# A hybrid encoder block with 32 experts: another order for the last two experts, a routing table built in groups, and shorter first loads

## What is computed

```python
u = rmsnorm(x, g_mix); z = u @ w_in
a = pool_mixer(z[..., :512]); s = ssm_mixer(z[..., 512:])      # pooling heads, S5 heads with a scan
h = x + concat([a, s]) @ w_out
# mixture of experts: 4 groups of 8, best group, then two experts of it, weights w1 and w2
v = rmsnorm(h, g_ffn); combine = route(v)
for e in range(32):
    hg = silu(v @ w_gate[e]) * (v @ w_up[e]) * combine[:, e]
    h = h + hg @ w_down[e]                                     # 1024 -> 256 -> 1024
gate = sigmoid(rmsnorm(h, g_ple) @ ple_gate_w + ple_gate_b)    # 1024 x 1024
h = h + gate * (p @ ple_proj_w)
out = rmsnorm(h, g_final)
```

## Time and profile before

| | us |
|---|---|
| three runs | 503.12, 504.16, 507.57 (median 504.16) |
| the profiled execution, its own time | 504.42 |
| its span, first to last instruction | 502.5 |
| TensorE busy | 471.3 (94%) |
| VectorE busy | 232.4 (46%) |
| ScalarE busy | 167.8 (33%) |
| GpSimd busy | 150.5 (30%) |
| mean granted TensorE clock | 0.993 of full speed |

### The profile page before, as it was taken

The page is one execution under the profiler, slowest core; times in us unless marked ns, Lnnn a source line. Parts: engine busy times, 40 slices in busy tenths (PEclk is TensorE's granted clock), DMA queues, the critical chain, the costliest instruction groups (busy, mean ns, idle before and its releaser), DMA issues.

```text
span 502.5 us, 7271 instructions
## 1 busy us (share of the span) xinstructions
PE 471.3 (94%) x2722; PEld 259.3 (52%) x2722; DVE 232.4 (46%) x683; ACT 167.8 (33%) x280; POOL 150.5 (30%) x136
## 2 busy tenths in 40 slices
PE   3899999999999999989999999998999997999993
PEld 3445564644944467655555555554554453444441
DVE  2899969999233348652222222221112111665525
ACT  5633657557342333111111111121212111214554
POOL 1069999925110001222222222211121210004350
PEclk9999999999999999999999999998999999999998
DMA  8884300599399976899999999999999999990022
GB/s 295 158 205 93 73 0 1 199 115 229 137 332 417 420 327 226 319 397 422 420 418 417 419 416 412 421 418 419 420 420 419 417 421 358 400 372 2 0 83 83
DMA packets 59659, 144.73 MB, mean 288 GB/s; under 512 B 26594, under 2 KB 36358, under 8 KB 47336
## 3 DMA queue, kind: packets, MB, share of 16 engines
q1 hardware_dynamic: 54024, 133.92, 72.3%
q0 software_dynamic: 5328, 10.31, 5.3%
q10 hardware_dynamic: 272, 0.04, 0.0%
HBM read 138.17 MB, written 14.19 MB: 303 GB/s over the span
## 4 chain that ended last, share of the span: by engine, by line
PE 69%; DMA 19%; SPq 4%; issue 3%; DVE 2%; ACT 1%; POOLq 0%; POOL 0%; DVEq 0%
PE bank L1666 63%; DMA ring<-in_exp_w_up_dram 12%; DMA moe<-v_d,gidx_all 4%; SPq L390 3%; PE bank L2079 2%; DMA pairs_d<-moe,sidx_all 1%; PE bank L1764 1%; DMA big<-pairs_d 1%; PE bank L2098 1%; PE bank L1936 1%; PE bank L2196 1%; SPq L395 1%; DVE h L1419 1%; ACT moe L558 1%; PE bank L1754 0%
## 5 line engine op out<-in xcount | busy, mean ns | idle before, releaser
L1666 PE MATMUL bank<-ring,moe 128*64 128x256 f32 (+2 forms) x848 | 110.8, 406 | 2.9 <-DMA ring<-in_exp_w_up_dram 2.5
L1666 PEld LDWEIGHTS bank<-ring,moe 128*64 128x64 f32 x848 | 60.2, 138 | 39.4 <-issue 14.4
L1592 POOL DMA_INDIRECT pairs_d<-moe,sidx_all x32 | 31.8, 993 | 150.4 <-ACT moe L558 78.2
L935 DVE TENSOR_TENSOR vrow<-moe,bank 64x128 f32<-64x128 f32 x64 | 18.6, 291 | 111.9 <-ACT moe L834 110.9
L1666 PE MATMUL bank<-ut,big 128*128 128x512 f32 x128 | 57.7, 597 | 1.4 <-ACT ut L570 1.4
L558 ACT ACTIVATE moe<-bank 128x512 f32<-128x512 f32 (+1 forms) x65 | 36.5, 582 | 62.3 <-PE bank L1666 52.2
L834 ACT ACTIVATE moe<-bank 64x256 f32<-64x256 f32 x32 | 12.1, 378 | 131.6 <-PE bank L1666 124.6
L1666 PE MATMUL bank<-ring,ut 128*128 128x512 f32 x128 | 55.7, 593 | 0.2 <-DVE ut L935 0.2
L1666 PE MATMUL bank<-big,moe 128*64 128x256 f32 (+1 forms) x264 | 41.8, 427 | 2.5 <-DMA big<-in_exp_w_up_dram 2.1
L935 DVE TENSOR_TENSOR ring<-ring,bank 128x64 f32<-128x64 f32 (+1 forms) x142 | 39.4, 278 | 2.8
L1666 PEld LDWEIGHTS bank<-ring,ut 128*128 128x128 f32 x128 | 24.0, 190 | 29.1 <-issue 29.1
(11 more groups left out here) (200 smaller groups left out, 607.9 us busy)
## 6 DMA issues: line engine op xcount, KB each, us to landing
ring<-in_exp_w_gate_dram SPq DMA_DIRECT2D x19, 1024.0 KB, 28.5
ring<-in_exp_w_down_dram SPq DMA_DIRECT2D x18, 1024.0 KB, 25.0
ring<-in_exp_w_up_dram SPq DMA_DIRECT2D x17, 1024.0 KB, 29.9
big<-in_exp_w_up_dram SPq DMA_DIRECT2D x7, 1024.0 KB
big<-in_exp_w_down_dram SPq DMA_DIRECT2D x7, 1024.0 KB, 15.1
big<-in_exp_w_gate_dram SPq DMA_DIRECT2D x6, 1024.0 KB
ut<-in_exp_w_up_dram SPq DMA_DIRECT2D x4, 1024.0 KB, 17.8
h<-in_exp_w_down_dram SPq DMA_DIRECT2D x4, 1024.0 KB, 27.8
```

The lines of the kernel that those rows point to most:

```text
L935: return dve.tensor_tensor(o, a, b, op)
L1592: pool.indirect_dma_start(pairs, bass.IndirectOffsetOnAxis(ap=index, axis=0), at(moe, ALL, M_Y + k * 512, [[1, 512]]), None, bounds_check= ...
L1666: return pe.matmul(o, a, b, start=start, stop=stop, skip_group_check=loose)
```

## The change

Head: the identity alone (128 columns) is loaded after the second tile of `x`, the other 497 columns of the constants after the second half of `w_in`, under `ld_win1`. C is turned after its own four loads; the vectors have a semaphore of their own and are turned after the next product. The filling of `tbl_d` and the cast of `pair_i` move behind the pooling loops on GpSimd.

Table: `table_groups()` stands after 3 slices of expert 0's gate-up product, with the operands exchanged (32 columns of `rh` are the weights, 128 of `oh` move) and four column groups of one bank as targets; VectorE copies the 128 x 128 result to memory, and `table_folded()`, after 5 slices, adds the four groups by one product with a 0/1 matrix. VectorE builds `oh` between its two copies of expert 0's rows. GpSimd takes the bounds of its indirect DMAs from two registers that are set once, before it waits for the indices.

Last experts and tail: see the diff.

```diff
-        ORDER = [(0, 0), (0, 1)] + [x for e in range(NE - 1) for x in ((e + 1, 0), (e + 1, 1), (e, 2))] + [(NE - 1, 2)]
+        ORDER = ([(0, 0), (0, 1)] + [x for e in range(NE - 2) for x in ((e + 1, 0), (e + 1, 1), (e, 2))]
+                 + [(NE - 2, 2), (NE - 1, 0), (NE - 1, 1), (NE - 1, 2)])
...
-                    sp.dma_start(cst[:, :], A["consts"]).then_inc(ld_c, 16)
+                    sp.dma_start(at(cst, ALL, C_ID, [[1, P]]), dr(A["consts"], C_ID, [[C_END, P], [1, P]])).then_inc(ld_c, 16)
...
+            def load_first_pairs(n):
+                sp.dma_start(at(big, ALL, n * 512, [[DM, 2], [1, 512]]),
+                             dr(pairs_d, n * 512, [[2 * DM, P], [DM, 2], [1, 512]])).then_inc(ld_late_half if n else ld_pairs[0], 16)
...
             sp.wait_ge(gu_ps, NE - 1)
             load_gate(0, 0, 4, ld_wple)
-            sp.wait_ge(moe_done, 1)
-            sp.wait_ge(gu_ps, NE)
-            load_pairs(0)
             sp.wait_ge(dn_ps, NE - 1)
             load_gate(0, 4, 4, ld_wple)
             load_h(1)
+            sp.wait_ge(moe_done, 1)
+            load_first_pairs(0)
+            load_first_pairs(1)
+            sp.wait_ge(gu_ps, NE)
             load_pairs(1)
...
-            x_out(0, xT_sb, 2, V_FB)
+            x_out(0, xT_sb, 2, V_FB, (0,))
             tt(qv("oh", ...), ...).then_inc(place_done, 1)
+            x_out(0, xT_sb, 2, V_FB, (1,))
...
             dve.wait_ge(tbl_ps, 1)
-            seq(dve.tensor_scalar(at(tblw, ALL, 0, [[1, NE]]), bank[6][:, 0:NE], float(EMPTY), None, ALU.add))
+            dve.tensor_copy(qv("pa", [[1, P]]), bank[7][:, 0:P]).then_inc(tbl_sb, 1)
+            dve.wait_ge(tbl_ps, 2)
+            seq(dve.tensor_scalar(at(tblw, ALL, 0, [[1, NE]]), bank[7][:, P:P + NE], float(EMPTY), None, ALU.add))
...
+            def first_half(n):
+                hv = at(h, ALL, n * 512, [[1, 512]])
+                if n:
+                    dve.wait_ge(ld_late_half, 16)
+                else:
+                    dve.wait_ge(ld_pairs[0], 32)
+                for k, col in enumerate((S_V, S_V + NT)):
+                    if k == 1:
+                        dve.wait_ge(comb, 3 * n + 1)
+                    dve.scalar_tensor_tensor(hv, at(big, ALL, k * DM + n * 512, [[1, 512]]), at(small, ALL, col, [[1, 1]]),
+                                             hv, ALU.mult, ALU.add).then_inc(comb, 1)
+                dve.wait_ge(cmb_ps, n + 1)
+                dve.wait_ge(comb, 3 * n + 2)
+                dve.scalar_tensor_tensor(hv, hv, at(small, ALL, S_ROOT2, [[1, 1]]), bank[n][:, :], ALU.mult, ALU.add
+                                         ).then_inc(comb, 1)
...
-            for t in range(2):
-                combine(t)
-                turned_g_ple(t)
-                inverse(S_RS3 + t, 1, NT + ROOT3[t])
+            first_half(0)
+            first_half(1)
+            turned_g_ple(0)
+            inverse(S_RS3, 1, NT + ROOT3[0])
+            combine(1)
+            turned_g_ple(1)
+            inverse(S_RS3 + 1, 1, NT + ROOT3[1])
...
-            pe.wait_ge(ld_craw, 16 * 10)
+            pe.wait_ge(ld_craw, 16 * 4)
...
+            def table_groups():
+                pe.wait_ge(place_done, 1)
                 for n in range(2 * NT):
-                    got = mm(bank[6][:, 0:NE], at(moe, ALL, Q["oh"] + n * P, [[1, P]]),
-                             at(moe, ALL, Q["rh"] + n * NE, [[1, NE]]), n == 0, n == 2 * NT - 1)
+                    g = n % NT
+                    got = mm(bank[7][g * NE:(g + 1) * NE, 0:P], at(moe, ALL, Q["rh"] + n * NE, [[1, NE]]),
+                             at(moe, ALL, Q["oh"] + n * P, [[1, P]]), n < NT, n >= NT, True)
                 got.then_inc(tbl_ps, 1)
+            def table_folded():
+                pe.wait_ge(tbl_sb, 1)
+                mm(bank[7][:, P:P + NE], at(moe, ALL, Q["pa"], [[1, P]]), at(cst, ALL, C_END, [[1, NE]]), True, True
+                   ).then_inc(tbl_ps, 1)
...
-            gu_step(0, table)
+            gu_step(0, {3: table_groups, 5: table_folded})
...
-            for e in range(1, NE):
+            for e in range(1, NE - 2):
...
-                if e + 1 < NE:
-                    gu_step(e + 1)
+                gu_step(e + 1)
...
+            h_step(NE - 2)
+            down_step(NE - 2)
+            pe.wait_ge(ppt_sb, 5)
+            pe.wait_ge(dn_sb, NE - 1)
+            combined_30(0)
+            combined_30(3)
+            gu_step(NE - 1)
+            h_step(NE - 1)
+            down_step(NE - 1)
...
-            for t in range(NT):
-                combined(t)
+            combined_31(0)
+            for t in (1, 2):
+                combined_30(t)
+                combined_31(t)
+            combined_31(3)
...
-            def gate(n):
+            def gate(n, between=None):
                 for j in range(KC):
+                    if between and j == 4:
+                        between()
...
-            turned_h(0)
+            turned_h(0, (0,))
             pe.wait_ge(ld_wple, 32)
             for t in range(NT):
-                gate(2 * t)
+                gate(2 * t, (lambda: turned_h(0, (1,))) if t == 0 else None)
```

More of the change, by code:

```diff
@@ L700, in _ @@
             zs_out(1)
+            act.wait_ge(c_ps, 3)
+            act.activation(at(vec, ALL, V_POOL, [[1, 28]]), bank[6][:, 0:28], ACT.Copy).then_inc(c_done, 1)
             wt_out(0, 0)
@@ L870, in _ @@
                 y_out(e)
+                if e + 2 == NE:
+                    silu(e + 1)
             with act.If(most(act) > CAP):
@@ L1429, in combine, with turned_g_ple @@
                                              ALU.mult, ALU.add).then_inc(comb, 1)
-            def turned_g_ple(t):
-                for n in range(2):
+            def turned_g_ple(t, halves=(0, 1)):
+                for n in halves:
                     dve.wait_ge(turned_ps, KC + 1 + NT + 2 * t + n + 1)
@@ L1501, in _ @@
             seq(pool.memset(fill[:, :], EMPTY))
-            pool.dma_start(dr(tbl_d, 0, [[P, P], [1, P]]), fill[:, :]).then_inc(tbl_filled, 16)
-            pool.wait_ge(ld_c, 32)
-            own.do(pool.tensor_copy(pair_i[:, :], at(cst, ALL, C_PAIR, [[1, 2 * NT]])))
             for off in (0, PAD + T):
@@ L1564, in _ @@
                 pool.wait_ge(diff_done, step + 1)
+            pool.dma_start(dr(tbl_d, 0, [[P, P], [1, P]]), fill[:, :]).then_inc(tbl_filled, 16)
+            own.do(pool.tensor_copy(pair_i[:, :], at(cst, ALL, C_PAIR, [[1, 2 * NT]])))
             for n in range(2 * NT):
@@ L2063, in slots, with combined_30, combined_31, x_rows @@
                 got.then_inc(ppt_ps, 1)
-            def combined(t):
+            def combined_30(t):
                 for n in range(2):
                     parts = (n * CAP, (n + 1) * CAP)
-                    for x in (NE - 2, NE - 1):
-                        turned = (at(ring, parts, E_S + t * P, [[1, P]]) if x == NE - 1 else
-                                  at(small, parts, S_S30 + t * P, [[1, P]]) if t < 2 else at(rw, parts, (t - 2) * P, [[1, P]]))
-                        got = mm(bank[2 * t + n][:, :], turned, at(moe, parts, M_Y + x % YBUF * 512, [[1, 512]]),
-                                 x == NE - 2, x == NE - 1, True)
-                    got.then_inc(cmb_ps, 1)
-            def x_rows(k):
+                    turned = at(small, parts, S_S30 + t * P, [[1, P]]) if t < 2 else at(rw, parts, (t - 2) * P, [[1, P]])
+                    mm(bank[2 * t + n][:, :], turned, at(moe, parts, M_Y + (NE - 2) % YBUF * 512, [[1, 512]]), True, False, True)
+            def combined_31(t):
+                for n in range(2):
+                    parts = (n * CAP, (n + 1) * CAP)
+                    mm(bank[2 * t + n][:, :], at(ring, parts, E_S + t * P, [[1, P]]),
+                       at(moe, parts, M_Y + (NE - 1) % YBUF * 512, [[1, 512]]), False, True, True).then_inc(cmb_ps, 1)
+            def x_rows(k, dst=(0, 6)):
                 for j in range(KC):
-                    last = pe.transpose(bank[j // 4 * 6][:, (j % 4) * P:(j % 4 + 1) * P],
+                    last = pe.transpose(bank[dst[j // 4]][:, (j % 4) * P:(j % 4 + 1) * P],
                                         at(moe, ALL, M_XG + k * DM + j, [[KC, P]]), ident)
@@ L2082, in x_rows, with gate_up @@
                         last.then_inc(xT_ps, 1)
-            def gate_up(k, odd, gate_w, up_w, dst, rows=0, between=None):
+            def gate_up(k, odd, gate_w, up_w, dst, rows=0, between={}):
                 for j in range(KC):
@@ L2088, in gate_up @@
                         pe.wait_ge(xT_sb, rows - 1 + j // 4)
-                    if between and j == 4:
-                        between()
+                    if j in between:
+                        between[j]()
                     for n, w in enumerate((gate_w, up_w)):
@@ L2095, in gate_up, with h_rows @@
                 return last
-            def h_rows():
-                return pe.transpose(bank[3][:, 0:P], vrow[:, :], ident)
+            def h_rows(col=0):
```

(8 more changed lines are left out.)

87 lines of the change are left out of this document (49 added, 38 removed).

## The result

The changed kernel takes 508.43 us (median of 9 runs, 507.64 to 510.06) beside 504.16 us before (9 runs, 502.91 to 507.57): the ratio of runs on one chip is 1.0053, with a 95% interval of 1.0028 to 1.0077. That is within 1% but clearly slower, and the median lies 4.7 us above the forecast and 2 us above its range. The two medians differ by 0.85%, more than the interval allows, and the runs of before scatter (502.57 to 508.56 over all chips, with medians of 506.1 to 506.4 on the three chips of the experiments); for sizes I use ratios and the profiled executions. These are 504.42 us before and 508.43 after, spans 502.5 and 506.4. The profiled execution of before is one of its faster ones: the ratio makes the loss 2.7 us, the two traces 3.9.

The account below looks back on a forecast made before the run. TensorE, busy 94% of the span, was taken as the bound, tied with the DMA engines from 225 to 410 us. 504.42 - 2.3 (head) + 1.85 (tail) = 503.97, or 503.7 for the median; range 501.0 to 506.4.

Parts of the forecast that it names:

- the sign of being wrong: Prediction counted wrong if gate(1), in the tail, starts before 443 or after 447 us in the new profile.
- Part 1: Start: shorter first loads bring ScalarE's chain 0.8 us sooner and C's turning 1.2 us sooner; ends -0.46 and -1.4.
- Part 2: Table in column groups: first gate-up product ends 1.1 us sooner (ends -1.4 and +0.3), the gather 1.1 us sooner.
- The changes of tiling mode: Table: two more TensorE drains would cut the gain by some 0.3 us; left out of the sum.
- What the head is worth later: Start and table together shift everything up to expert 30 by -2.3 us; ends -1.0 and -3.
- Rival 3: Start and table give only -1.0 us while the tail's 1.85 us loss stands: 505.0 us; chance 0.15.
- Part 3: Last two experts: the new order buys nothing; combined products end at 434.5 us, against 433.9 before.
- Part 4: Tail: the wait inside gate(0) and late combine(1) delay gate(1), +1.85 us; ends +1.0 and +2.6.
- The landing of the pairs' first half: Tail: with the queue's dip at 423 to 426 us counted as empty, the half lands at 430.3 us.
- rival 2: Tail: pairs land late, holding VectorE, 1 us per us after 430.7; 506.0 us at landing 433, 509.5 at 436.5; chance 0.2.
- A gate slice is two instructions of 0.43: Tail: the first four slices of gate(0) take 3.44 us, ending at 439.5 us.
- The wait in the middle: Gate(0), before slice 4: TensorE must wait for VectorE and turn the second half, 1.53 us.

Follow-up runs that it names:

- e12: The changed kernel run once more, unaltered: 508.13 us, ratio 1.0047 to the kernel before.
- e11: e1 with the second half of the gate weights and v of tile 1 issued ahead of the pairs: 509.79 us, ratio 1.0106 (4 runs).
- e7: The kernel before with only the shorter first loads and split waits of the start: 503.65 us, ratio 0.9964.
- e8: The kernel before with only the table in groups and the gather's bounds in registers: 503.77 us, ratio 0.9957.
- e1: The changed kernel's start and table, with the old order of experts and the old tail: 502.36 us, ratio 0.9938 to the kernel before.
- e3: The changed kernel with the pairs issued ahead of the second half of the gate weights and v of tile 1: 504.57 us, ratio 0.9979.
- e4: The changed kernel with both halves of tile 0 turned ahead of the first gate product: 504.51 us, ratio 0.9989.
- e5: The changed kernel with expert 31's last combined product moved behind the first transposes, into TensorE's idle: 506.33 us, ratio 1.0019.
- e6: e1 with the new order of the last two experts, the old loads and turning of tile 0 kept: 502.85 us, ratio 0.9941.
- e9: The changed kernel with the edits of e3 and e4 together: 502.97 us, ratio 0.9938.
- e2: The kernel before with the new order of experts and the new tail, old start and table: 509.93 us, ratio 1.0091.
- e10: e1 with expert 30's first combined product put into TensorE's wait for expert 31's output: 502.71 us, ratio 0.995.

## Why the prediction was wrong

The forecast for an execution like the profiled one was 503.97; it took 508.43. Put into the times of the new profile, the prediction had gate(1) start at 446.3 - 2.3 = 444.0, and the chain has it at 448.45. It named a start after 447 as the sign of being wrong. By its steps:

**Part 1, half confirmed.** I took -1.2 by giving ScalarE the whole 0.8 us of the shorter load. It got 0.22; the wait for the third tile only moved. C's turning came 0.85 sooner, 0.46 of it the wait for the vectors, which vanished. Executions differ: in e12, the same kernel, C is turned at 24.38, 1.23 sooner, and the third tile is started on 0.61 sooner. Over the traces with the shorter first loads C's turning comes 0.66 (e11) to 1.37 us (e7) sooner, so -1.2 lies inside.

**Part 2, confirmed and a little low.** The products took 0.64 (0.7 predicted), the fold 0.41 (0.15), and the product ended 1.85 us sooner, of which 0.9 was there at its start, so the table itself gave 1.0 where I had 1.1. The gather came 2.1 sooner, 2.3 predicted: of this the step between indices and gather gave 0.7 and not 0.5. e7 and e8 give both parts their worth in time. The changes of tiling mode did leave something. The 12 and the 8 instructions ahead of the two blocks take 1.44 and 1.01 us (202.68 to 204.12, 204.70 to 205.71), where 0.107 each is 1.28 and 0.86, and neither block waits for an operand there. That is 0.3 us, an estimate, which the prediction had worked out and left out of its sum; no run takes the switches alone. GpSimd's gain of 0.7 is that of one edit, which puts the bounds into registers and also moves two waits for the stores of `v` ahead of the wait for the indices; e8 does not part the two.

**What the head is worth later.** I had -2.3 at the experts. Expert 30's hidden row is turned 1.3 us sooner (414.48 for the 415.78 of the earlier trace rows). The issue of the pairs, which follows the last scatter, varies more between executions: against the 424.89 of the earlier trace rows it came 1.5 us sooner here, and 1.4 to 2.3 in the traces of e1, e3, e4, e5, e6 and e12. In e12, a second execution of the changed kernel, the hidden row is at 413.81 and the issue at 422.74, 2.0 and 2.1 us sooner: -2.3 was too much by 0.3 to 1.0. In time the head gave 0.62% (e1), 3.1 us of 506. Rival 3, that the head gives half, did not come out.

**Part 3, confirmed.** TensorE waited 1.12 us for vrow of expert 31 (1.4 predicted) and no longer for its up weights; the combined products ended at 433.4, 434.7 in old times, for the predicted 434.5. The 0.6 us that the new order costs are 0.7 in e6 against e1.

**Part 4 is where it failed**, in two steps.

*The landing of the pairs' first half was mis-sized.* "Landing 430.3", in old times; it was 431.16 in the new, 432.5 in old times by the 1.3 us of the head. From the old issue at 424.89 that was to be 5.4 us, and it was 7.7. I had let the queue be empty at the dip and counted the 1.57 MB to 427.2, 2.3 us behind the issue, then 1.3 and 1.7. e3, with nothing ahead, takes 3.75 for the last two, and the 1.57 MB add 4.0. The dip has no room for them: over its four slices (340, 225, 178, 225 in the earlier trace rows) 420 GB/s would have moved some 0.7 MB more, an estimate. In the changed kernel the queue does not run dry at all (same slices as the earlier trace rows, 389, 399, 375 and 393 from 423 to 427):

```profile
GB/s 451 393 426 418 442 418 410 434 410 447 401 418 410 434 410 414 426 406 412 410 387 401 387 389 399 375 393 393 418 420 383 412 391 385 389 389 391 393 410 418
```

The prediction's own rival 2 had the mechanism, the place (VectorE before `turned_g_ple(0)`) and the point from which it decides (430.7), so it came out in part: 1.8 us of it. e3 and e11 show the mechanism from both sides: taking the 1.57 MB away makes the landing 4.0 us faster, and putting them ahead makes it 4.1 slower. The earlier trace rows give 12.2 us as the median landing of the four pair loads; I used that in the rival only, and in the sum the 6.29 of the one load that stood in front of the others. (12.2 us from the issue at 424.89 end at 437.1, not at the 436.5 of the rival.)

*"A gate slice is two instructions of 0.43. After four slices (3.44 ...)" took a duration from a product that had never waited.* Nowhere in the working did I ask what TensorE's clock would do behind the idle which the late pairs, and VectorE's six instructions in one piece, would leave. The four slices took 5.21. e5 isolates this term at 1.7 us by filling the idle with work that was there anyway.

The rest of the part held. The wait in the middle was 1.38 us (1.53 predicted), combine(1) was late, and gate(1) started 5.1 us after the second four slices did (443.19 to 448.29, the first instruction; 5.3 predicted). TensorE's idle between the two fours was 0.78 (1 predicted). VectorE's before it was 5.99, 4 predicted, and takes in the slower slices.

The sum of the miss at gate(1), predicted 444.0 and found 448.3 by the timeline: gate(0) started at 436.60 and not 433.75, +2.85 (head 1.0 less than I had there, the rest landing and VectorE); clock +1.77; middle wait -0.15; from slice 4 to gate(1) -0.2. Together 4.27. In e12 gate(1) starts at 447.64.

**Against before**, gate(0) starts at the same time (436.60 for 436.63): the landing and the new order ate what the head had won. The 3.84 us that follow are clock 1.8, the wait with the second half's transposes 1.4 and, by difference, the late combine(1) 0.7.

**Which version is best.** e1, e6 and e9 (502.4 to 503.0) are about 0.6% faster than before and 1.1% faster than the changed kernel, and among themselves their intervals overlap. The head is what is worth keeping; the new order gains nothing, and the split tail only comes back to the same place once both repairs are made. I would keep e1, the smallest edit of the three.

**Left open.** Why e7 and e8 together show 0.79% where e1 has 0.62% can't be told from noise. e11's four runs give its size loosely. VectorE does all six instructions on the pairs before it writes the first half of `ut`, though that half is turned at 434.27 and `ut` comes at 435.77; another order there was not tried. What fixes the 3.2 to 4.4 us between the landings of the two halves of the pairs in e3 and e9, issued back to back with 1.3 us of bytes each, was not tried. What decides whether the clock falls behind an idle of some 2 to 2.7 us is not known.

## What to carry to other kernels

Before putting a load ahead of another on one queue, write down what bytes then stand in front of the one that the tail waits for: it is late by their transfer, about 4 us for 1.57 MB here, also where the queue looked idle. Where TensorE will stand in one piece, as in the 2.3 us here, price the work behind the idle at half the clock as well as the idle itself, or break the idle with work that has to be done anyway: four instructions moved without any new transfer gave back 1.7 us. And before splitting work into halves, ask whether the second half is ready when the first is used up: here it cost a wait of 1.4 us, with its transposes, and in none of the runs did the split beat the kernel without it (e1).

## What was not expected of the hardware

TensorE's granted clock fell to half in the tail behind idles of 2.34, 2.33, 2.33 and 3.56 us (changed, e2, e12, e11), in a kernel whose TensorE is 93% busy, and stayed at 1.00 behind 1.64, 1.28 and 0.88 (e4, e5, e3).

The rest of the traces shows that this is no rule. TensorE also waits for up weights at about 344 us, and there the kernel before has a fall itself, behind 2.24 us, while e4 has none behind 2.65. TensorE's timeline of 340 to 349 us and a stretch behind it, of the kernel before:

```profile
345.30 3.91 PE L1666 MATMUL bank<-ring,moe 128*64 128x256 f32 x20 [2.24 <-DMA ring<-in_exp_w_up_dram]
346.00:348.00 2.00, 2.00 (x12) 1.05 (x12) 0.00 (x0) 0.00 (x0) 0.00 (x0) 0.50 1.02 420
```

The same of e4:

```profile
343.50 3.67 PE L1708 MATMUL bank<-ring,moe 128*64 128x256 f32 x32 [2.65 <-DMA ring<-in_exp_w_up_dram]
344.00:346.00 2.00, 2.00 (x22) 1.36 (x20) 0.00 (x0) 0.00 (x0) 0.00 (x0) 1.00 1.01 420
```

The changed kernel, e3, e5, e8 and e12 fell there behind 2.62 to 2.65 us, e2 and e9 did not behind 2.61 and 2.63. Ahead of expert 31's gate-up product e7, e10 and e11 fell behind 2.12, 2.19 and 2.12 us, and before, e1 and e8 did not behind 2.09, 2.17 and 2.12. From 205 us to the end of the gate products every fall stands beside an idle of 1.92 us or more, and none beside a shorter one. Such falls go with the scatter of the times too: on the chip of e9 to e12, the runs of before with a mean granted clock of 0.988 or less took 506.1 to 508.6 us, those with 0.993 or more 502.6 to 506.5.

Nor does a fall show at one fixed place. In the changed kernel's stretch 434 to 436, where TensorE worked 0.26 us of 2, the row still says 1.00, and the 0.50 comes at 438 to 440, when the engine is busy again. In e12 the row of 434 to 436, with no work in it, has 0.94 already.

With the bounds of the indirect DMA in registers and the waits for `v` ahead of the wait for the indices, the gather starts 0.01 us after the last index, where there had been 0.7. I had guessed the smaller part of it.
